# Delta rule: odd heads placed across the partition halves

## The reference

```python
def step(S, xs):
    rt, wt, kt, vt, kkt, bt = xs
    sa = jnp.einsum('bhvk,bhk->bhv', S, kkt)
    S = S * wt[:, :, None, :] - sa[..., None] * bt[:, :, None, :] + vt[..., None] * kt[:, :, None, :]
    return S, jnp.einsum('bhvk,bhk->bhv', S, rt)
```

## Time and profile before

| | |
|---|---|
| median of 3 runs | 1035.37 us (1032.6 to 1037.3) |
| profiled execution | 1035.65 us, span 1033.8 us |
| TensorE matmul busy | 921.1 us, 89% of the span |
| VectorE busy | 484.5 us, 47% |
| ScalarE busy | 282.2 us, 27% |
| mean granted TensorE clock | 0.967 of full speed |

### The profile page before, as it was taken

One profiled execution on the slowest core, in us unless ns is written; L12 is line 12 of the kernel. 1 busy time (PEld: TensorE's weight loads), 2 busy tenths in 40 slices (PEclk: granted clock), 3 DMA queues, 4 the chain that ended last, 5 costly groups with the idle time before them and its releaser, 6 DMA issues. The chain is left out here.

```text
span 1033.8 us, 25458 instructions
## 1 busy us (share of the span) xinstructions
PE 921.1 (89%) x11037; PEld 651.4 (63%) x11037; DVE 484.5 (47%) x1371; ACT 282.2 (27%) x655; POOL 61.8 (6%) x92
## 2 busy tenths in 40 slices
PE   7899998996799989979989999899688989997696
PEld 4455557665677875635765555766676887663365
DVE  1362288665664443112636228866686261311035
ACT  3330308433221521110143030843331161111000
POOL 0000000000000021012000000000000002000120
PEclk9899999998899999989999999999999999998999
DMA  9859624412246999999761311441206799999992
GB/s 372 359 144 277 179 82 158 171 36 93 90 178 273 422 401 347 376 378 396 320 234 60 113 46 41 154 175 37 92 10 252 309 382 326 367 374 357 391 416 81
DMA packets 43654, 239.51 MB, mean 232 GB/s; under 512 B 5136, under 2 KB 8336, under 8 KB 19984
## 3 DMA queue, kind: packets, MB, share of 16 engines
q1 hardware_dynamic: 30192, 197.42, 49.2%
q0 software_dynamic: 9504, 34.08, 10.8%
q10 hardware_dynamic: 3840, 6.29, 1.9%
HBM read 211.03 MB, written 26.74 MB: 230 GB/s over the span
## 5 line engine op out<-in xcount | busy, mean ns | idle before, releaser
L1103 PE MATMUL bank<-sb_hT,sb_ring 128*128 128x385 f32 (+1 forms) x640 | 208.9, 496 | 4.4 <-ACT sb_hT L1873 4.4
L1103 PEld LDWEIGHTS bank<-sb_hT,sb_ring 128*128 128x128 f32 (+1 forms) x640 | 116.8, 189 | 91.6 <-issue 12.1
L1873 ACT ACTIVATE sb_u<-bank 128x256 f32<-128x256 f32 (+4 forms) x136 | 58.2, 456 | 249.9 <-PE bank L1103 239.1
L1103 PE MATMUL bank<-sb_arena 64*64 64x64 f32 (+5 forms) x1032 | 96.8, 333 | 11.1 <-DMA sb_arena<-weights 6.4
L1103 PE MATMUL bank<-sb_ring,sb_arena 128*64 128x256 f32 (+4 forms) x672 | 80.9, 370 | 1.5 <-DVE sb_ring L2252 0.7
L1103 PEld LDWEIGHTS bank<-sb_arena 128*64 128x64 f32 (+2 forms) x1032 | 55.5, 145 | 38.8 <-issue 18.7
L2255 DVE SCALAR_TENSOR_TENSOR sb_xT<-bank,sb_mod,sb_xT 128x128 f32<-128x128 f32 (+1 forms) x160 | 46.4, 351 | 57.9 <-PE bank L1103 57.7
L1103 PEld LDWEIGHTS bank<-sb_ring,sb_arena 128*64 128x64 f32 (+2 forms) x672 | 56.2, 150 | 23.9 <-issue 14.6
L1103 PE MATMUL bank<-sb_u,sb_arena 64*64 64x64 f32 (+2 forms) x744 | 57.9, 325 | 12.3 <-DMA sb_u<-weights 6.5
L1103 PE MATMUL bank<-sb_o,sb_ring 128*128 128x128 f32 (+2 forms) x320 | 66.0, 361 | 0.0
L1873 ACT ACTIVATE sb_tmp<-bank 128x128 f32<-128x128 f32 x35 | 9.7, 278 | 194.1 <-PE bank L1103 194.1
(11 more groups left out here) (241 smaller groups left out, 1299.5 us busy)
## 6 DMA issues: line engine op xcount, KB each, us to landing
sb_ring<-weights SPq DMA_DIRECT2D x95, 1024.0 KB, 9.3
sb_arena<-weights SPq DMA_DIRECT2D x40, 1024.0 KB, 18.2
sb_u<-weights SPq DMA_DIRECT2D x22, 1024.0 KB, 10.8
sb_hT<-weights SPq DMA_DIRECT2D x10, 1024.0 KB, 21.5
sb_sq<-weights SPq DMA_DIRECT2D x8, 1024.0 KB, 20.3
x_slots<-sb_o POOLq DMA_DIRECT2D x1, 6912.0 KB, 40.1
sb_consts<-weights SPq DMA_DIRECT2D x6, 1024.0 KB, 23.3
sb_sq<-x_slots POOLq DMA_DIRECT2D x17, 256.0 KB, 8.1
```

What stands on the lines that cost most here:

```text
L1103: return nc.tensor.matmul(out, lhsT, rhs, start=start, stop=stop, skip_group_check=True)
L1873: return nc.scalar.activation(out, in_, func, **kw)
```

## The change

The odd heads (j = 1, 3) of the inverses, right-hand sides and values are kept in the other partition half than the even heads.

- `merge0`'s second product is made by the new `sixteen_by`, which uses all four quadrants: even heads of both batches go to bank 0 from a half to the same half, odd heads of both to bank 1 from a half to the other. VectorE copies the even heads of both batches, ScalarE the odd ones, to `invT_all`.
- `cross1` places its heads so that `merge1` finds left and right side in the same half; `merge1` pairs them with `place`.
- `values(q)` and `solve(q)` fill two banks, even heads and odd heads, with four quadrants. ScalarE copies `values` in two instructions (128x128 each). `solve`'s even heads are copied by ScalarE, its odd heads by VectorE; `state` and `output` wait for both.
- `carry(q)` puts its odd half's result in the other half.

Two groups are added to the bank plan for each q.

```diff
             elif step == "values":
-                g("a", "rv", l, b)
+                for odd in range(2):
+                    g("a", "rv", l, b, odd)
...
             elif step == "solve":
-                g("a", "x", l, b)
+                for odd in range(2):
+                    g("av"[odd], "x", l, b, odd)
...
-            def eight(bank, at, lhsT, rhs):
-
+            def sixteen_by(turned, banks_, lhsT, rhs):
+
+                last = [None, None]
                 for j in range(4):
-                    for q in HALVES:
-                        last = mm(bank[q, at + 64 * j:at + 64 * j + 64], lhsT[q, j, :], rhs[q, j, :])
+                    for m in sorted(range(2), key=lambda m: turned(m, j)):
+                        for i, q in enumerate(HALVES):
+                            k = turned(m, j)
+                            at = 64 * (2 * m + j // 2)
+                            last[k] = mm(banks_[k][HALVES[(i + k) % 2], at:at + 64], lhsT[m][q, j, :], rhs[m][q, j, :])
                 return last
...
-                    for ins in sixteen(banks_, 0, [g4[m][:, :, 2, :] for m in pair], inv):
+                    left = [g4[m][:, :, 2, :] for m in pair]
+                    for ins in sixteen_by(lambda m, j: (m + j) % 2, banks_, left, inv) if k else sixteen(banks_, 0, left, inv):
...
-                    for m in range(2):
-                        eight(banks_[m], 0, cross[m], invT[pair[m]]).then_inc(psum_filled, 1)
+                    for ins in sixteen_by(lambda m, j: j % 2, banks_, cross, [invT[m] for m in pair]):
+                        ins.then_inc(psum_filled, 1)
...
-                    for ins in sixteen(banks_, 0, cross, [invT[m] for m in pair]):
+                    for ins in sixteen(banks_, 0, cross, [invT[m] for m in pair], place=lambda m, j: j ^ m):
...
+                turned = lambda d, j: HALVES[(chunks[d] + j) % 2]
...
-                            last = mm(bank[side, 64 * j:64 * j + 64], g4[batches[d]][side, j, 0, :],
+                            at = 64 * (j // 2)
+                            last = mm(banks_[j % 2][turned(d, j), at:at + 64], g4[batches[d]][side, j, 0, :],
                                       rv_tm[side, j // 2, tiles[d], p])
...
-                                last = mm(banks_[half][side, i * 64:i * 64 + 64],
+                                last = mm(banks_[half][turned(d, half), i * 64:i * 64 + 64],
...
-                            last = mm(bank[side, 64 * j:64 * j + 64], invT[batches[d]][side, j, :], rhs[side, j, :])
-                    last.then_inc(psum_filled, 1)
+                            rows_, at = turned(d, j), 64 * (j // 2)
+                            last = mm(banks_[j % 2][side, at:at + 64], invT[batches[d]][rows_, j, :], rhs[rows_, j, :])
+                            if j >= 2 and d:
+                                last.then_inc(psum_filled, 1)
...
                 elif step == "values":
-                    copy(r_values[b], "rv", l, b)
+                    for odd in range(2):
+                        copy(r_values[b][:, odd::2, :], "rv", l, b, odd)
                 elif step == "solve":
-                    copy(x_sol, "x", l, b)
+                    copy(x_sol[:, 0::2, :], "x", l, b, 0)
...
+                elif step == "solve":
+                    bank = filled(dve, "x", l, q, 1)
+                    v.tensor_copy(x_sol[:, 1::2, :], shaped(bank[:, 0:P], 2, 64)).then_inc(read("x", l, q, 1), 1)
```

More of the change, by code:

```diff
@@ L664, in program @@
         inv = [carve(tail, 4, 64) for _ in range(2)]
-        invT = [carve(tail, 4, 64) for _ in RW_BATCHES]
-        cross = [carve(spare, 4, 64) for _ in range(2)]
+        invT_all = carve(tail, len(RW_BATCHES), 4, 64)
+        invT = [invT_all[:, b, :, :] for b in range(len(RW_BATCHES))]
+        cross_all = carve(spare, 2, 4, 64)
+        cross = [cross_all[:, m, :, :] for m in range(2)]
         r_values = [carve(tail, 4, 64) for _ in range(CHUNKS)]
@@ L1298, in attention, with sixteen @@
                             fill(l, f"pv{t}")
-            def sixteen(banks_, at, lhsT, rhs, turned=(0, 1)):
+            def sixteen(banks_, at, lhsT, rhs, turned=(0, 1), place=lambda m, j: j):
                 for j in range(4):
@@ L1498, in recurrence_step @@
                 if step == "values":
-                    bank = open_bank(pe, "rv", l, q)
+                    banks_ = [open_bank(pe, "rv", l, q, odd) for odd in range(2)]
                     for d in range(2):
@@ L1521, in recurrence_step @@
                 elif step == "solve":
-                    bank = open_bank(pe, "x", l, q)
+                    banks_ = [open_bank(pe, "x", l, q, odd) for odd in range(2)]
                     for d in range(2):
                         taken(pe, "tt", l, batches[d], 1)
-                    taken(pe, "rv", l, q)
+                    taken(pe, "rv", l, q, 1)
                     if q:
@@ L1540, in recurrence_step @@
                                rv_tm[side, i, tiles[d], p], i == 0, False)
-                    taken(pe, "x", l, q)
+                    for odd in range(2):
+                        taken(pe, "x", l, q, odd)
                     for j in range(4):
@@ L2121, in rwkv_step @@
                     copy(inv[1], "t", l, b + 1, 5)
-                    copy(invT[b + 1], "tt", l, b + 1, 0)
+                    bank = filled(act, "tt", l, b + 1, 0)
+                    f(invT_all[:, b:b + 2, 1::2, :], shaped(bank[:, 0:256], 2, 2, 64), ACT.Copy).then_inc(read("tt", l, b + 1, 0), 1)
                 elif step == "merge1":
@@ L2597, in inverse_step @@
                         bank = filled(dve, "cross", l, b + m, k)
-                        tt(cross[m], four(bank), bc(mask, 1, 4), ALU.mult).then_inc(read("cross", l, b + m, k), 1)
+                        if k:
+                            tt(cross_all[:, :, m::2, :], shaped(bank[:, 0:256], 2, 2, 64), bc(bc(mask, 1, 2), 1, 2), ALU.mult)\
+                                .then_inc(read("cross", l, b + m, k), 1)
+                        else:
+                            tt(cross[m], four(bank), bc(mask, 1, 4), ALU.mult).then_inc(read("cross", l, b + m, k), 1)
                 elif step == "merge0":
@@ L2602, in inverse_step @@
                     bank = filled(dve, "tt", l, b, 0)
-                    v.tensor_copy(invT[b], four(bank)).then_inc(read("tt", l, b, 0), 1)
+                    v.tensor_copy(invT_all[:, b:b + 2, 0::2, :], shaped(bank[:, 0:256], 2, 2, 64)).then_inc(read("tt", l, b, 0), 1)
                 elif step == "merge1":
@@ L2611, in recurrence_step @@
                 if step == "carry":
-                    taken(dve, "rv", l, q)
+                    taken(dve, "rv", l, q, 1)
                     for half in range(2):
```

2 lines of the change are left out of this document (1 added, 1 removed).

## The result

The changed kernel takes 1040.8 us in the median of 20 runs (1034.6 to 1045.2), the kernel before 1037.2 us beside it: ratio 1.0039, 95% interval 1.0024 to 1.0054. It is slower by 0.4%. The forecast was no change (1035.2, range 1030 to 1040.5).

A forecast was written before the change was run, and what follows sets the result against it. TensorE and VectorE were taken to bound the touched stretches in turn. Steps summed to -0.09 us a layer, -0.2 in two, giving 1035.2 us from a median of 1035.37; own range 1033 to 1037.5, wide range 1030 to 1040.5.

The forecast's parts named there:

- Prices of the groups: TensorE alone: values and solve from 0.68 to 0.46 us each, merge0's second product from 1.10 to at best 0.68.
- row-half rival: Two row halves exclude each other in a bank, so TensorE's gains fall away: 1037.3 us, chance 0.03.
- Steps 2 and 6: Layer 1, solve(0) and solve(2): VectorE's new copy delays power3's product and state, +0.15 and +0.30 us.
- steps 4 and 7: Layer 1, solve(1) with its merge0, and solve(3): VectorE's new copy delays the masks, +0.12 and +0.22 us.
- Steps 3 and 5: values(1) saves time, -0.22 us; at values(2) the right-hand side waits for ScalarE's copy, +0.08 us.
- Step 1: merge0 of batches 0 and 1: of 0.42 us only 0.18 is saved, as cross1 cannot start before ScalarE's copy.
- Step 8: Layer 1, solve(4): right-hand side 0.08 us later, solve 0.22 and the copy 0.10 shorter, -0.24 us.
- step 9: Layer 1, solve(5): solve and its copy shorter, without a later start, -0.32 us.
- the copy 0.10 shorter: After solve, ScalarE copies 128x128 in 0.28 us instead of 128x256 in 0.38 or 0.39.
- What PE is given it spends on waiting for DVE: Delta-rule stretches: TensorE's gains are taken back by waits for VectorE, -0.2 us in two layers; chance 0.55.
- A cost that no arithmetic on work shows: TensorE's instruction refills fall elsewhere in the delta-rule stretches; each stall gained or lost is worth 2.5 to 4.5 us.
- one refill stall more: Delta-rule stretches: one more late refill of TensorE's instructions than now, about 1038.5 us, chance 0.10.

The follow-up runs named there:

- e13: Changed kernel with ScalarE copying both banks of a pair in one instruction and TensorE waiting once per pair: 1036.5 us, 4.6 +- 0.9 us back against the changed kernel.
- e18: Kernel before with values and solve in two banks, two quadrants, joint ScalarE copy, one wait per pair; e13 differs from it by +0.3 +- 1.0 us.
- e17: e13 with TensorE waiting for both banks of solve again, 24 waits more: 5.5 +- 1.0 us slower than e13, +5.1 us against the kernel before.
- e2: Changed kernel repeated unchanged, with a second, more typical profile: span 1041.7 us; the changed kernel with this repeat has a mean of 1041.1 +- 0.5 us.
- e15: Kernel before with solve in two banks on two quadrants, both copied by ScalarE: 2.1 +- 1.0 us slower than the same with VectorE copying one bank.
- e7: Changed kernel without those TensorE waits that an earlier wait already implies: 3.6 +- 0.9 us faster than the changed kernel.
- e8: Changed kernel with both banks of solve copied by ScalarE and the implied TensorE waits left out: among the ten runs with means of 1035.9 to 1038.6 us.
- e14: e13 with TensorE's implied waits left out: not better than e13, among the ten runs with means of 1035.9 to 1038.6 us.
- e9: Kernel before with 64 empty instructions at the start of TensorE's program: time stayed where it was, among the ten runs with means of 1035.9 to 1038.6 us.
- e1: Kernel before repeated unchanged, with a second profile; over all calls the kernel before has a mean of 1036.7 +- 0.2 us.

## Why the prediction was wrong

No change was forecast, and the kernel became slower by 0.4%: inside the 0.5% that had a chance of 0.74, but 3.3 us beyond the forecast's own range and 0.3 beyond the wide one.

- **Prices of the groups: right,** `merge0` 0.69 us, `values` and `solve` 0.46, but 0.64 for a `solve` with a block's edge in it. The row-half rival is refuted.
- **Steps 2, 4, 6, 7: right in place and sign.** Steps 2 and 6 are in the rows above; in steps 4 and 7 VectorE's copy (743.27 and 769.34 in the profile after) stands ahead of the masks (743.47 and 769.54), as forecast. VectorE's copies have PE wait 1.7 us in layer 0 and 2.0 in layer 1. Steps 3 and 5 I have not measured.
- **Step 1: mis-sized.** -0.18 was forecast, -0.01 measured (0.91 to 0.90 us from `merge0`'s second group to `cross1`, for the first pair of either layer). PE starts 0.24 us behind the end of ScalarE's copy (219.72), with two semaphore instructions between, and not 0.07: it waited for that copy before the change too.
- **Steps 8 and 9: mis-sized.** Step 8's way from `solve(4)` to the state update saved nothing (1.73 and 1.74 us) where 0.32 was forecast, for the two reasons given with the rows. In step 9 `solve` is 0.22 us shorter, but the term "the copy 0.10 shorter" measured 0: it is 0.53 us from ScalarE's copy (782.44) to PE's next group (782.97), as before. With steps 1, 8 and 9 so mis-sized, layer 1 is about 0.6 us slower than its sum. In layer 0 step 8 fared better, since the edge inside `solve(4)` was there before (0.88 us) and not after (0.46). So the path through the copies can account for less than 1 us of the loss.
- **"What PE is given it spends on waiting for DVE": not the main reason.** e13 takes VectorE out of the copies altogether and keeps the quadrants, and gains 0.2 +- 0.8 us on the kernel before; e18 against e13 prices the quadrants at nothing within 1.0 us. What their shorter groups are spent on instead is open.
- **The step that failed is "A cost that no arithmetic on work shows".** It named the mechanism (added PE waits move the refills), kept it out of the forecast with a value of zero and shared its chance evenly between a gain and a loss. That cost was nearly the whole result. The runs put the added waits at the size of the loss, and leave open how far they act through the refills: 24 always satisfied waits cost 5.5 +- 1.0 us (e17 against e13), and 4.6 +- 0.9 come back where the joint copy removes them (e13). The rival "one refill stall more", 1038.5 us with a chance of 0.10, came nearest. "Issue" was forecast near 13 us and is 15.7 in the trace after and 18.2 in e2, in more and shorter waits (15 and 16 instead of 8), 0.9 us of either being the two waits for VectorE's sum. That is less than the 5 us by which the prediction would have called itself wrong. The lower granted clock, which goes with some 2 us, had no term.
- **Settled and open.** Shown: the loss hangs on TensorE's added waits; copies, banks, VectorE and quadrants are at most a small part (e13, e15, e17, e18), and the stalls stand at block edges. Argued only: that the moved edges are how 24 waits cost 5.5 us. Of e17's loss its profile shows 5.2 us more "issue" in layer 0 and 1.6 us at the output projection (5.29 instead of 3.71), but the waits of other kinds shrink by some of it, and the sum of "issue" does not sort the kernels: e7, e8 and e14 have 18.1, 20.2 and 20.9 us, the last the most of all, without being slow. No run moved the edges alone.

## What to carry to other kernels

In a stretch of small matmuls ask first how many TensorE instructions stand between two fetch stalls and what they take: if a block goes at the pace of the fetch, faster matmuls there may be worth nothing. Count added wait instructions as a cost even where they are always satisfied: 24 were worth 5.5 us here. When a result is split over two banks, copy neighbouring banks in one instruction and wait once. Read the sum of "issue" before a change that adds instructions, and check in the trace that an experiment which should move something has moved it.

## What the runs showed that I had not expected

- 24 waits of TensorE that are always satisfied cost 5.5 +- 1.0 us (e17 against e13).
- One ScalarE copy of 128x256 reads two banks in 0.38 us, as it does one.
- Each semaphore instruction between a copy and the matmul that needs it puts PE's start off by about 0.10 us (0.15 with one, 0.25 with two), whichever engine copied.
- 64 or 128 nops at the program's start left the places of the fetch stalls unchanged (e9: 4804 and 6339, as before).
- The clock fell right behind the 2.7 us stall that ended at 274.17 in e17: 0.66 granted in the 5 us window above. The kernel before has such a place too, 0.50 granted from 275.70 to 279.10, behind its stall of 2.5 us. At 1.2 GHz for a part of it the output projection took 5.4 instead of 3.7 us (e2); there PE had waited 1.5 us for weights, and e1, with the same wait, kept its clock.
